# Moving operands of the matrix products start at other byte offsets than the weights

## The chip, the cores and the metric

The kernel runs on one core of a Trainium2 chip. The metric is the device time of one execution in microseconds (us); lower is better. Before the change two runs took 3464.58 and 3474.01 us, median 3469.3.

## The reference

Two networks run one after the other on a sequence of 512 tokens of width 1024, in float32. The first has four layers, each a token mixer (a gated linear recurrence, a gated unit that mixes chunks of 128 tokens, a short convolution, and the recurrence again) and a squared-ReLU MLP of width 4096. The second has one layer: a projection that feeds a delta-rule recurrence in chunks of 64 tokens and a dilated attention, then cross-attention over 256 memory rows, then another squared-ReLU MLP. What most of the time goes to is this:

```python
def _sqrelu_mlp(h, w1, w2):
    return jnp.square(jax.nn.relu(h @ w1)) @ w2
...
        h = _rmsnorm(x, norm_mix_g[i])
        ...
        x = x + mix
        x = x + _sqrelu_mlp(_rmsnorm(x, norm_mlp_g[i]), mlp_w1[i], mlp_w2[i])
...
        n = rmsnorm(h, norm_mix_g[l])
        proj = (n @ w_in[l]).astype(f32)
        ...
        u = rmsnorm(h, norm_ffn_g[l]) @ ffn_w1[l]
        h = h + (jnp.square(jax.nn.relu(u)) @ ffn_w2[l]).astype(h.dtype)
```

## The kernel before

Activations stay in SBUF, features on the 128 partitions and the 512 tokens along the row: `x` is the residual stream, 8 tiles of 128 features by 512 tokens. Every large product is made of three: weights and activations are each split into an upper part in the type float32r and the rest, also float32r, and the kernel adds upper*upper, upper weights*lower activations and lower weights*upper activations in PSUM. The upper and lower parts of the weights are `wh` and `wl`; those of the normed input are `xh` and `xl`, those of the MLP's activation `hh` and `hl`. Other inputs of products have pairs of their own: `yh`/`yl` (mixer outputs), `mh`/`ml` (memory), `rh`/`rl`, `oh`/`ol`, `gdh`/`gdl`, `yah`/`yal`.

Weights come in units of 1024 rows by 256 columns. SyncE's queue brings a unit into one of two slots of `raw` (L422), ScalarE rounds it to `wh` (L433), VectorE subtracts to get `wl` (L438), and TensorE multiplies (L501): for each of 8 row tiles and 2 column tiles one instruction for each of the three products, so 48 to a unit. In each, 128x128 weights are loaded into the array, and 512 columns of the activation stream past them. A few stages are swapped (L476): the activation is loaded, and 256 columns of the weights stream past it. Loads and streams are separate instructions; the load for the next product runs beside the stream of this one. Semaphores order everything: `landed`, `upper`, `lower` and `units` for the weights' two slots, `split` for activation tiles as they become ready, `evac` for PSUM banks.

After a stage of the kind `fin` VectorE adds PSUM to `x` (L671), ScalarE writes a tile of `xh` (L594), and VectorE one of `xl` (L681). After a stage of the kind `relu` VectorE writes `tmp` (L660), POOL squares it into `hf` (L617), ScalarE squares it into `hh` (L584), and VectorE writes `hl` (L666). Groups that repeat run as loops in which a register holds the tile's address.

Memory is laid out by hand. `pers` (L101) places tensors one after another, from `raw` to `c128`; `at` (L140) places tensors at offsets in KiB from `ARENA` (L137), which is moved up to the offset of the weights modulo 512 bytes. `xh` and `xl` are persistent, and their space is also that of the chunked recurrence, by `XH_AT`. As all the tensors from `wh` to `xl` have sizes that are multiples of 512 bytes, and a row tile of an activation is 2048 bytes, every float32r operand on either side of a product begins at the same byte modulo 512 in this kernel. Behind `tmp`, whose 4160 bytes are 8 x 512 + 64, the small tensors of the list (`hf` is the first of them) stand at other offsets.

Of the kernel before, what the change touches and what calls it, by code (L numbers as in the profile page):

```python
# [10 lines left out]
F32R = mybir.dt.float32r  # L11

P = 128
T = 512
D = 1024
ND = D // P
# [8 lines left out]
NC = T // CH  # L25
NH2 = 8
MEM = 256
NEG = 1e30
KIB = 1024
# [65 lines left out]
def build(nc, a, out):  # L95
# [5 lines left out]
    def pers(name, shape, dt=F32):  # L101

        n = 4
        for s in shape[1:]:
            n *= s
        off = used[0]
        used[0] += (n + 31) // 32 * 32
        return nc.alloc_sbuf_tensor_at(name, shape, dt, offset=off)
# [8 lines left out]
    wl = pers("wl", [P, 2, 8, 256], F32R)  # L117
    x = pers("x", [P, ND, T])
    XH_AT = used[0]
    xh = pers("xh", [P, ND, T], F32R)  # L120
    xl = pers("xl", [P, ND, T], F32R)
    ident = pers("ident", [P, P])
    ones = pers("ones", [P, P])
    headones = pers("headones", [P, P])
# [6 lines left out]
    prm = [pers(f"prm{i}", [P, P]) for i in range(4)]  # L131
# [8 lines left out]
    def at(name, kib, shape, dt=F32, base_at=None):  # L140
        n = 4
        for s in shape[1:]:
            n *= s
        off = (ARENA if base_at is None else base_at) + int(kib * KIB)
        assert base_at is not None or off + n <= LIMIT, (name, off + n, LIMIT)
        return nc.alloc_sbuf_tensor_at(name, shape, dt, offset=off)


    hh = at("hh", 0, [P, 16, T], F32R)
    hl = at("hl", 32, [P, 16, T], F32R)  # L150
    yh = at("yh", 40, [P, NR, T], F32R)
    yl = at("yl", 60, [P, NR, T], F32R)
    xtok = at("xtok", 0, [P, 4, D])
# [45 lines left out]
    w2a2 = at("w2a2", 88, [P, D])  # L199
    wda = at("wda", 92, [P, T])  # L200
    PCt = at("PC", 94, [P, NC, NH2])
    PCs = at("PCs", 94.25, [P, NC, NH2])
    XT_AT = XH_AT - 16 * KIB
    rt = at("rt", 0, [P, 8, T], base_at=XT_AT)

# [37 lines left out]
    stx = at("stx", 92, [P, 2, 16])  # L243
    mjunk = at("mjunk", 73, [P, D])

    fo = at("fo", 64, [P, ND, T])

    ps = [ctx.enter_context(nc.psum_tensor(f"ps{i}", [P, T], F32)) for i in range(8)]

# [2481 lines left out]
```

## Time and profile before

| | |
|---|---|
| two runs | 3464.58 and 3474.01 us, median 3469.3 |
| the profiled execution | span 3463.6 us, from the first to the last instruction; a time of its own beside the span isn't given, the lower run is 1.0 us above it |
| TensorE (PE) busy | 3370.7 us, 97% |
| weight loads (PEld) busy | 2754.4 us, 80% |
| VectorE, ScalarE, POOL busy | 1764.5, 1162.7 and 467.8 us |
| mean granted TensorE clock | 0.992 of full |
| DMA | 329.56 MB, mean 95 GB/s |

TensorE's matrix instructions are pipelined, so the time that one "takes" in the profile overlaps the next one, and TensorE is called busy throughout. What tells how fast it works is the distance from the start of one instruction to the start of the next. The timeline shows starts to 0.01 us, so this document takes them over many instructions.

### The profile page before, as it was taken

Reading aid. Unit: us, or ns where it says so; the run is one execution under the profiler, and the core shown is the slowest. Engines: PE = TensorE matmul, PEld = TensorE weight load, DVE = VectorE, ACT = ScalarE, POOL = GpSimd, SP = SyncE. Lnnn points to the kernel's source line nnn. Section 1 sums busy time; section 2 is a strip of 40 time slices with the busy share of each in tenths; the row PEclk is TensorE's granted clock in tenths of the full one; section 3 lists DMA queues with packets and bytes.
Section 4 is the critical chain, followed back from the end, with each engine's and each line's share of the span. In section 5 each row is a group of like instructions: output and inputs, shape, how many; then the busy total and the mean of one; then the engine's idle time right before and its main releaser. Section 6 shows DMA issues by size and latency. Waiting matters only on the chain. (4 is left out here: it accounts for less than half of the span.)

```text
span 3463.6 us, 51738 instructions
## 1 busy us (share of the span) xinstructions
PE 3370.7 (97%) x21556; PEld 2754.4 (80%) x21556; DVE 1764.5 (51%) x1954; ACT 1162.7 (34%) x1455; POOL 467.8 (14%) x417
## 2 busy tenths in 40 slices
PE   7999999999999999999999999999998889999998
PEld 5588888888888888887588888788776878878887
DVE  7764343454344554345765253655686555555342
ACT  3532123432222232222532123334563543332122
POOL 2011011020011021011011012000141221111011
PEclk9999999999999999999999999999999999999999
DMA  4233333233322233233233323343332122313232
GB/s 131 72 105 99 97 97 97 86 97 97 97 97 86 96 101 105 87 103 109 69 98 97 98 96 109 102 133 115 100 96 91 41 65 86 122 61 100 94 98 72
DMA packets 313270, 329.56 MB, mean 95 GB/s; under 512 B 22786, under 2 KB 304389, under 8 KB 312581
## 3 DMA queue, kind: packets, MB, share of 16 engines
q1 hardware_dynamic: 306325, 303.39, 27.6%
q0 software_dynamic: 4464, 19.40, 1.7%
q10 hardware_dynamic: 2304, 4.20, 0.3%
q8 instruction: 137, 2.24, 0.3%
q14 instruction: 40, 0.33, 0.0%
HBM read 312.28 MB, written 14.68 MB: 94 GB/s over the span
## 5 line engine op out<-in xcount | busy, mean ns | idle before, releaser
L501 PE MATMUL ps<-xh,wh 128*128 128x512 f32 x2360 | 930.6, 394 | 10.5 <-DVE wl L438 10.5
L501 PE MATMUL ps<-xh,wl 128*128 128x512 f32 x2360 | 920.1, 390 | 0.0
L501 PE MATMUL ps<-xl,wh 128*128 128x512 f32 x2360 | 919.7, 390 | 0.0
L438 DVE TENSOR_TENSOR wl<-raw,wh 128x2048 fp32r<-128x2048 f32 (+2 forms) x281 | 634.0, 2256 | 423.0 <-ACT wh L433 422.3
L433 ACT ACTIVATE wh<-raw 128x2048 fp32r<-128x2048 f32 (+1 forms) x284 | 526.9, 1855 | 668.7 <-PE ps L501 641.8
L501 PEld LDWEIGHTS ps<-xh,wh 128*128 128x128 f32 x2360 | 444.1, 188 | 115.9 <-issue 22.8
L501 PEld LDWEIGHTS ps<-xl,wh 128*128 128x128 f32 x2360 | 444.1, 188 | 95.2 <-issue 4.3
L501 PEld LDWEIGHTS ps<-xh,wl 128*128 128x128 f32 x2360 | 443.7, 188 | 93.1
L501 PE MATMUL ps<-hh,wh 128*128 128x512 f32 x1280 | 498.5, 389 | 1.2 <-DVE wl L438 0.9
L501 PE MATMUL ps<-hh,wl 128*128 128x512 f32 x1280 | 498.0, 389 | 0.0
L501 PE MATMUL ps<-hl,wh 128*128 128x512 f32 x1280 | 498.0, 389 | 0.0
L617 POOL TENSOR_TENSOR hf<-tmp 128x512 f32<-128x512 f32 x160 | 163.3, 1042 | 1133.6 <-DVE tmp L660 1133.6
L584 ACT ACTIVATE hh<-tmp 128x512 f32 (+1 forms) x160 | 97.7, 633 | 598.7 <-DVE tmp L660 598.7
L501 PEld LDWEIGHTS ps<-hh,wh 128*128 128x128 f32 x1280 | 240.3, 188 | 52.3 <-DVE wl L438 2.4
L501 PEld LDWEIGHTS ps<-hh,wl 128*128 128x128 f32 x1280 | 240.3, 188 | 50.0
L501 PEld LDWEIGHTS ps<-hl,wh 128*128 128x128 f32 x1280 | 240.3, 188 | 49.6
L660 DVE SCALAR_TENSOR_TENSOR tmp<-ps,rs 128x512 f32<-128x512 f32 x160 | 103.0, 686 | 341.2 <-PE ps L501 341.1
L671 DVE TENSOR_TENSOR x<-x,ps 128x512 f32 (+1 forms) x128 | 82.2, 684 | 355.8 <-PE ps L501 355.8
L630 POOL TENSOR_TENSOR acc<-acc,hf 128x512 f32<-128x512 f32 x80 | 118.4, 1480 | 1016.7 <-ACT hf L596 1012.8
L666 DVE TENSOR_TENSOR hl<-hf,hh 128x512 f32 (+1 forms) x160 | 158.4, 1029 | 55.4 <-POOL hf L617 55.4
L594 ACT ACTIVATE xh<-x,prm (+1 forms) x72 | 51.6, 717 | 273.0 <-DVE x L671 273.0
L501 PE MATMUL ps<-yh,wh 128*128 128x512 f32 x352 | 137.4, 390 | 0.0
(426 smaller groups left out, 3680.2 us busy)
## 6 DMA issues: line engine op xcount, KB each, us to landing
raw<-in_mlp_w SPq DMA_DIRECT2D x128, 1024.0 KB, 5.4
raw<-in_ffn_w SPq DMA_DIRECT2D x32, 1024.0 KB, 5.2
raw<-in_w_in SPq DMA_DIRECT2D x31, 1024.0 KB, 5.3
raw<-in_a_w_in SPq DMA_DIRECT2D x20, 1024.0 KB, 5.1
raw<-in_c_w_in SPq DMA_DIRECT2D x12, 1024.0 KB, 5.1
raw<-in_a_w_out SPq DMA_DIRECT2D x16, 640.0 KB, 4.0
raw<-in_b_w_in SPq DMA_DIRECT2D x8, 1024.0 KB, 5.7
raw<-in_xa_wkv SPq DMA_DIRECT2D x8, 1024.0 KB, 6.0
```

The costliest lines, as they stand in the source:

```text
L433: nc.scalar.activation(wh[:, p.slot(su), 0:n], raw[:, p.slot(su), 0:n], ACT.Copy).then_inc(upper, 1)
L438: nc.vector.tensor_tensor(wl[:, p.slot(su), 0:n], raw[:, p.slot(su), 0:n], wh[:, p.slot(su), 0:n], ALU.subtract).then_inc(lower, 1)
L501: last = nc.tensor.matmul(banks[mt][:, 0:st.n], stat_, ops[oi][at_, kk, 0:st.n], start=k == 0 and su == 0 and n_ == 0, stop=k == kb - 1 an ...
L584: nc.scalar.activation(hh[:, bass.ds(t, 1)], tmp[:, mt:mt + 1, 0:T], ACT.Square).then_inc(acted, 1)
L594: nc.scalar.activation(xh[:, bass.ds(t, 1)], x[:, bass.ds(t, 1)], ACT.Copy, scale=gaincol(st, t)).then_inc(acted, 1)
L617: nc.gpsimd.tensor_tensor(hf[:, mt], tmp[:, mt, 0:T], tmp[:, mt, 0:T], ALU.mult).then_inc(pooled, 1)
L630: nc.gpsimd.tensor_tensor(acc[:], acc[:], sq[:, mt], ALU.add).then_inc(pooled, 1)
L660: nc.vector.scalar_tensor_tensor(out=tmp[:, mt, 0:T], in0=ps[b + mt][:], scalar=0.0, in1=rs[:], op0=ALU.max, op1=ALU.mult).then_inc(evac, 1)
L666: nc.vector.tensor_tensor(hl[:, bass.ds(t, 1)], hf[:, mt:mt + 1], hh[:, bass.ds(t, 1)], ALU.subtract).then_inc(split, 1)
L671: nc.vector.tensor_tensor(xt, xt, ps[b + mt][:].rearrange("p (a n) -> p a n", a=1), ALU.add).then_inc(evac, 1)
```

## The change

`xh` starts 256 bytes, `xl` 16, `hh` 32 and `hl` 384 bytes past the weights' offset modulo 512. To make room, the space of `xh` and `xl` grows by 544 bytes; what stands behind it in the list moves up by 544 bytes (32 modulo 512), and the arena by 512. `PCs`, a small table of the recurrence, moves into columns of `prm3` that nothing uses, and `fo`, the tensor of the final norm, up by 1 KiB. Sizes, arithmetic, semaphores and the number of products are untouched; `yh`, `yl` and the other pairs keep their offset modulo 512.

```diff
--- before.py
+++ after.py
@@ -117,8 +117,11 @@
     wl = pers("wl", [P, 2, 8, 256], F32R)
     x = pers("x", [P, ND, T])
     XH_AT = used[0]
-    xh = pers("xh", [P, ND, T], F32R)
-    xl = pers("xl", [P, ND, T], F32R)
+    OFF = dict(xh=256, xl=16, hh=32, hl=384)
+    xspace = pers("xspace", [P, 2 * ND * T + (512 + 32) // 4], F32R)
+    xh = nc.alloc_sbuf_tensor_at("xh", [P, ND, T], F32R, offset=XH_AT + OFF["xh"])
+    xl_space = nc.alloc_sbuf_tensor_at("xl", [P, OFF["xl"] // 4 + ND * T], F32R, offset=XH_AT + ND * T * 4 + 512)
+    xl = xl_space[:, OFF["xl"] // 4:OFF["xl"] // 4 + ND * T].rearrange("p (k t) -> p k t", t=T)
     ident = pers("ident", [P, P])
     ones = pers("ones", [P, P])
     headones = pers("headones", [P, P])
@@ -146,8 +149,8 @@
         return nc.alloc_sbuf_tensor_at(name, shape, dt, offset=off)
 
 
-    hh = at("hh", 0, [P, 16, T], F32R)
-    hl = at("hl", 32, [P, 16, T], F32R)
+    hh = at("hh", OFF["hh"] / KIB, [P, 16, T], F32R)
+    hl = at("hl", 32 + OFF["hl"] / KIB, [P, 16, T], F32R)
     yh = at("yh", 40, [P, NR, T], F32R)
     yl = at("yl", 60, [P, NR, T], F32R)
     xtok = at("xtok", 0, [P, 4, D])
@@ -199,7 +202,7 @@
     w2a2 = at("w2a2", 88, [P, D])
     wda = at("wda", 92, [P, T])
     PCt = at("PC", 94, [P, NC, NH2])
-    PCs = at("PCs", 94.25, [P, NC, NH2])
+    PCs = prm[3][:, 64:P].rearrange("p (c q) -> p c q", c=NC)
     XT_AT = XH_AT - 16 * KIB
     rt = at("rt", 0, [P, 8, T], base_at=XT_AT)
 
@@ -243,7 +246,7 @@
     stx = at("stx", 92, [P, 2, 16])
     mjunk = at("mjunk", 73, [P, D])
 
-    fo = at("fo", 64, [P, ND, T])
+    fo = at("fo", 65, [P, ND, T])
 
     ps = [ctx.enter_context(nc.psum_tensor(f"ps{i}", [P, T], F32)) for i in range(8)]
 
```

Instructions on TensorE, ScalarE, POOL and SyncE are the same, in the same order. `xl` is now a slice that begins 16 bytes inside its tensor, and on VectorE this adds one register instruction for each of its writes in loops, 28 in the program, each of which runs twice. The place is the end of the loop body of a stage of the kind `fin`, on VectorE, before:

```order
L671 TENSOR_TENSOR x<-x,ps 128x512
L671 ISA
L671 TENSOR_TENSOR x<-x,ps 128x512
L676 REGISTER_ALU
L681 ISA
L681 SCALAR_TENSOR_TENSOR xl<-x,prm_62,xh 128x512
L676 REGISTER_ALU
L681 ISA
L681 SCALAR_TENSOR_TENSOR xl<-x,prm_62,xh 128x512
```

and in the changed kernel (lines are 3 further down):

```order
L674 TENSOR_TENSOR x<-x,ps 128x512
L674 ISA
L674 TENSOR_TENSOR x<-x,ps 128x512
L679 REGISTER_ALU
L684 ISA
L684 REGISTER_ALU
L684 SCALAR_TENSOR_TENSOR xl<-x,prm_63,xh 128x512
L679 REGISTER_ALU
L684 ISA
L684 REGISTER_ALU
L684 SCALAR_TENSOR_TENSOR xl<-x,prm_63,xh 128x512
```

A `REGISTER_ALU` now stands between the register work of L684 and the `SCALAR_TENSOR_TENSOR` that writes `xl`, in both halves of the body; nothing else moved.

## Rows read from the trace of the kernel before

**Rows 1.** The page: its head and the busy time of each engine.
```profile
span 3463.6 us, 51738 instructions
PE 3370.7 (97%) x21556; PEld 2754.4 (80%) x21556; DVE 1764.5 (51%) x1954; ACT 1162.7 (34%) x1455; POOL 467.8 (14%) x417
```

**Rows 2.** Waits of PE: line, releaser, total us, times, longest us.
```profile
PE ps L501 <- DVE wl L438: 14.5, 8, 3.1
...
PE ps L476 <- DVE xl L681: 1.8, 2, 1.1
```

**Rows 3.** Groups of PE by shape: busy us, mean ns, idle before.
```profile
L501 PE MATMUL ps<-xh,wh 128*128 128x512 f32 x2360 | 930.6, 394 | 10.5 <-DVE wl L438 10.5
...
L501 PE MATMUL ps<-xl,wh 128*128 128x512 f32 x2360 | 919.7, 390 | 0.0
L501 PE MATMUL ps<-hh,wh 128*128 128x512 f32 x1280 | 498.5, 389 | 1.2 <-DVE wl L438 0.9
...
L476 PE MATMUL ps<-wh,xh 128*128 128x256 f32 x224 | 64.9, 290 | 6.8 <-DVE wl L438 5.0 <-DVE xl L681 1.8
```

**Rows 4.** Timeline of PE, 28 products in a row: start us, duration us.
```profile
499.67 0.39 PE L501 MATMUL ps<-hl,wh 128*128 128x512 f32 x1
...
505.79 0.39 PE L501 MATMUL ps<-hl,wh 128*128 128x512 f32 x1
```

**Rows 5.** Timeline of PE, 15 swapped products of 256 columns in a row.
```profile
624.77 0.28 PE L476 MATMUL ps<-wh,xl 128*128 128x256 f32 x1
...
626.45 0.28 PE L476 MATMUL ps<-wh,xh 128*128 128x256 f32 x1
```

**Rows 6.** Timeline of PE at the lower clock, and its window (PEclk third last).
```profile
649.13 0.63 PE L501 MATMUL ps<-xh,wh 128*128 128x512 f32 x1
...
650.41 0.60 PE L501 MATMUL ps<-xh,wh 128*128 128x512 f32 x1
...
649.50:650.40 0.90, 0.90 (x3) 0.67 (x2) 0.00 (x0) 0.90 (x1) 0.00 (x0) 0.50 1.09 387
```

**Rows 7.** Timeline of PE after another product, at the higher clock, and its window.
```profile
124.62 0.39 PE L501 MATMUL ps<-xl,wh 128*128 128x512 f32 x1
...
125.08 0.40 PE L501 MATMUL ps<-xh,wh 128*128 128x512 f32 x1
125.32 0.39 PE L501 MATMUL ps<-xl,wh 128*128 128x512 f32 x1
125.54 0.39 PE L501 MATMUL ps<-xh,wl 128*128 128x512 f32 x1
...
126.93 0.39 PE L501 MATMUL ps<-xh,wl 128*128 128x512 f32 x1
...
129.19 0.39 PE L501 MATMUL ps<-xh,wh 128*128 128x512 f32 x1
...
124.70:129.40 4.70, 4.70 (x22) 3.86 (x21) 3.94 (x7) 4.65 (x7) 0.00 (x0) 1.00 0.52 179
```

**Rows 8.** Timeline of PE: plain float32 products, one and fifteen merged.
```profile
3046.43 0.59 PE L2342 MATMUL ps<-ptx,vx 128*128 128x512 f32 x1
...
3047.73 6.60 PE L2342 MATMUL ps<-ptx,vx 128*128 128x512 f32 x15
```

**Rows 9.** Line L1604: duration min/median/max ns, first and last start us.
```profile
L1604 PE MATMUL ps<-rt,headones x8: 590/590/591, 2491.8 to 2607.2; 128*128 128x512 f32 x8
...
L1604 PE MATMUL ps<-hf,headones x8: 590/590/591, 2510.3 to 2624.9; 128*128 128x512 f32 x8
```

**Rows 10.** What feeds a unit: groups of ACT and DVE, and DMA issues.
```profile
L433 ACT ACTIVATE wh<-raw 128x2048 fp32r<-128x2048 f32 x264 | 504.2, 1910 | 652.7 <-PE ps L501 626.3 <-DMA raw<-in_a_w_in 13.8 <-PE ps L476 11.7
...
L438 DVE TENSOR_TENSOR wl<-raw,wh 128x2048 fp32r<-128x2048 f32 x261 | 603.5, 2312 | 411.7 <-ACT wh L433 411.0
...
raw<-in_mlp_w SPq DMA_DIRECT2D x128, 1024.0 KB, 5.4
```

**Rows 11.** Line L681, its register instructions: duration min/median/max ns.
```profile
L681 DVEq FUSED_REGOPS  x56: 80/80/86, 519.3 to 3101.4; - x56
```

## The prediction, made before the changed kernel was run

> **What bounds the kernel now.** I read the page's busy times first: TensorE is busy 97% of the span, VectorE 51% [rows 1]. The waits of TensorE come next. The largest on another engine in the steady stages is 14.5 us in eight pieces, for a split of weights [rows 2], so nothing but its own pace holds TensorE up. What it works on is in the groups by shape: the streams of `xh` and `hh` [rows 3], each of which stands there three times with the same count (upper*upper, upper*lower, lower*upper). Durations of 390 ns overlap there, so the pace has to be read from starts. In the timeline 27 steps from 499.67 to 505.79 us [rows 4] give 0.2267 us for a product of 512 columns, and 14 steps from 624.77 to 626.45 [rows 5] give 0.1200 us for one of 256. The difference is 106.7 ns for 256 columns, 0.417 ns each, which is the upper level of the clock, 2.4 GHz. So 512 columns stream in 213.3 ns, 256 in 106.7, and in both cases **13.3 ns are left over for each product**. These are all the change can speak to.
>
> Three rows say what kind of time that is. At the lower clock (1.2 GHz, granted 0.50) three steps from 649.13 to 650.41 make 0.427 us each [rows 6], exactly 512 columns and nothing over. Plain float32 products come at (6.60 - 0.59)/14 = 429.3 ns [rows 8], twice 213.3 and 2.6 over: they ask for the stream at half the rate and lose next to nothing. And the left-over isn't constant. When the stream starts again behind another stage, at full clock (granted 1.00), ten steps from 124.62 to 126.93 us take 231 ns each, single ones between 0.22 and 0.24, and only then do they settle, with ten steps of 226 from 126.93 to 129.19 [rows 7]. The operands and their addresses modulo 512 are the same before and after settling. A fixed price of changing weights would not wander. Something depends on how the load of the next weights and the running stream meet in time, and it ends in a locked rhythm at 226.7.
>
> That is the question of this change: whether they also meet by address. If so, new offsets move the rhythm to which it locks. If they meet by time alone, nothing changes.
>
> **The change, part by part.** Products touched: 3 x 2360 with `xh` and `xl` and 3 x 1280 with `hh` and `hl`, of 512 columns, 10,920 in all, and 3 x 224 = 672 swapped ones [rows 3]. They take 10,920 x 0.2267 + 672 x 0.120 = 2475 + 81 = 2556 us, 74% of the span. Each ns on all 11,592 is 11.6 us. One per cent is 3 ns; 2%, 69 us, is 6.0 ns. About 2% is also what a measurement of this kernel can tell from no change, and I use it as that.
>
> It passes through in full both ways. A unit of weights is 48 products, 10.9 us; its supply is 5.4 us of transfer, 1.9 of ScalarE and 2.3 of VectorE [rows 10], in two slots. The last two, which follow the release of a slot, take 4.2 us while the other slot is multiplied. Even at 213.3 ns a unit would last 10.2 us, and the same slack would cover them.
>
> The price of the new offsets for a product isn't in this trace, since no float32r product here has another. Bounds: the slowest and fastest single steps of the same products, 0.24 and 0.22 us [rows 7], which are +13.3 and -6.7 ns on the settled pace (+154 and -77 us in all). Beyond the fast end lies the left-over of the plain float32 product, 2.6 instead of 13.3 ns, worth 10.7 x 11,592 = 124 us. I take 0. The nearest row on address is L1604: its stream of `rt` begins at the weights' offset and that of `hf` 64 bytes past it (4160 bytes of `tmp` are 8 x 512 + 64), and both take 590 ns, minimum to maximum within 1 ns [rows 9]. It is a weak row, for these are plain float32, which lose little anyway. The second reason is the 13.3 ns themselves: the same for streams of 512 and 256 columns [rows 4, 5], in which `xh` is once the stream and once what is loaded. A clash by address would have to cost the same in both roles and at both lengths.
>
> The Trainium skill (TensorE: Matmul & The Clock Gate, "Step-by-step: what each phase is for") says that TensorE reads its stream and its weights through two independent ports of SBUF, so that loading the next weights takes nothing from the running product; by that rule offsets can't matter either, and the time stays. The same page ("Back-to-back issue gap") puts products of 512 columns 215.8 ns apart, with which the trace does not agree: 226.7 [rows 4], so the rule of independent ports does not explain the left-over either.
>
> The rest costs nothing. VectorE runs 28 x 2 = 56 more register instructions; the nearest, 80 ns each [rows 11], would make 4.5 us, below it 0. They hide in VectorE's idle half, and TensorE waits for `xl` only twice, 1.8 us [rows 2]; uncovered there, they add 0.2 us. `xh`, `xl`, `hh` and `hl` are written at new offsets; if that slowed ScalarE or VectorE, the tiles' slack before the eighth row tile (7 x 6 x 0.227 = 9.5 us into the next stage) covers it. The small tensors move by 32 bytes, the arena by 512, `PCs` and `fo` elsewhere; the products on them are plain float32, for which rows 9 stand.
>
> Sum: 3463.6 + 0. The median of the runs is 5.7 us above that span, the lower run 1.0; I forecast **3468 us**.
>
> **Rivals.**
> 1. *No effect of address*, the forecast, chance 0.46. For it: rows 9, and one left-over for two lengths and roles. Against: the wandering of rows 7.
> 2. *The rhythm locks at a worse place*, slower. Place: the stream of every product in rows 3, beside the load of the next weights. In the mild form the products run as before they settle, 231 ns: +4.3 x 11.6 = +50 us, 3519, chance 0.15. In the hard one they lock at the slow end, 0.24: +154 us, 3624, chance 0.12. It decides from 6 ns on average, that is 233. For it: the unsettled steps are slower on average than the settled ones, so a place taken blindly is likelier worse than better. Four different offsets average out, against the hard form.
> 3. *It locks at a better place.* Between 0.22 and the present pace: down to -77 us, in the middle -39 us, 3431, chance 0.15, a third of it beyond 2%. For it: a step of 0.22 exists.
> 4. *The meeting goes away*, and the left-over falls to 2.6 ns: 3468 - 124 = 3344, chance 0.12. For it: rows 6 and 8 show that it vanishes once the stream asks for less, so it isn't needed for changing weights. Against: four unlike offsets would all have to be good ones.
>
> Likely enough too is a mixture, one operand better and one worse; it lies between these.
>
> **How the numbers follow.** Within 2%: 0.46 + nearly all of the mild slow form (0.13) + two thirds of rival 3 (0.10) = 0.69. Faster by over 2%: 0.12 + 0.05 = 0.17. Slower by over 2%: 0.12 + 0.02 = 0.14. The range goes from 3375, which leaves most of rival 4 out (0.10), to 3550, which leaves most of the hard slow form out (0.10). The forecast's own range is 3455 to 3482.
>
> **What would show it.** The distance between starts for each kind of stream: `xh` (256), `xl` (16), `hh` (32), `hl` (384), and `yh` as one that keeps its offset. If rival 1 is right, all are at 226.7, and the steps of rows 7 repeat. If address counts, `yh` stays at 226.7 and others leave it, each for itself; then the kernel's time must move by the sum of their counts times their differences. A swapped product of 256 columns tells whether it counts which side is offset. If the time moves while all distances stay, I am wrong in another way: then waits of TensorE for `wl` or `xl` must have grown beyond rows 2. What would make the prediction wrong is mainly that the left-over is a meeting by address, which this trace can't exclude.

## The result

The changed kernel took 3511.03 and 3512.88 us, median 3511.95, against 3469.3 before: ratio 1.0127, 95% interval 1.0109 to 1.0146. It is 1.3% slower, 43 us. None of the executions of the kernel before that were timed beside the experiments took more than 3476.24 us, so this is clear of noise. The forecast was 3468, no change; what came is nearest to rival 2 in its mild form, which had 3519.

The page of the changed kernel says at once what it is not:

```profile
span 3509.3 us, 51794 instructions
PE 3420.2 (97%) x21556; PEld 2751.8 (78%) x21556; DVE 1767.8 (50%) x1954; ACT 1162.7 (33%) x1455; POOL 470.4 (13%) x417
```

Compared with [rows 1] TensorE is busy 49.5 us longer with the same number of products, and the other engines are within 3.3 us of what they were. The groups of TensorE by shape (busy us, mean ns of one, idle before):

```profile
L504 PE MATMUL ps<-xh,wh 128*128 128x512 f32 x2360 | 939.0, 398 | 9.4 <-DVE wl L441 9.2
L504 PE MATMUL ps<-xl,wh 128*128 128x512 f32 x2360 | 930.4, 394 | 0.0
L504 PE MATMUL ps<-hl,wh 128*128 128x512 f32 x1280 | 504.8, 394 | 0.0
L504 PE MATMUL ps<-hh,wh 128*128 128x512 f32 x1280 | 502.0, 392 | 0.7 <-DVE wl L441 0.7
L504 PE MATMUL ps<-yh,wh 128*128 128x512 f32 x352 | 137.5, 391 | 0.0
```

All four streams that moved are 3 to 5 ns longer than in [rows 3], and than the row of `hl` in the same view of the kernel before:

```profile
L501 PE MATMUL ps<-hl,wh 128*128 128x512 f32 x1280 | 498.0, 389 | 0.0
```

The wait for the split of weights has not grown (9.2 us before `xh`, 10.5 in [rows 3]). The starts tell the pace. In the timeline of `xh` and `xl`, 24 products apart, then of `hh` and `hl`, 21 apart (start us, duration us):

```profile
1319.79 0.39 PE L504 MATMUL ps<-xl,wh 128*128 128x512 f32 x1
...
1323.27 0.39 PE L504 MATMUL ps<-xl,wh 128*128 128x512 f32 x1
...
1325.35 0.40 PE L504 MATMUL ps<-xl,wh 128*128 128x512 f32 x1
```
```profile
503.06 0.39 PE L504 MATMUL ps<-hl,wh 128*128 128x512 f32 x1
...
507.90 0.40 PE L504 MATMUL ps<-hl,wh 128*128 128x512 f32 x1
```

That is 5.56/24 = 0.2317 and 4.84/21 = 0.2305 us, where [rows 4] had 0.2267. The first stretch lies deep inside a stage, long after the ten or so products in which the kernel before settled [rows 7]; the second begins with the second product of its stage. The changed kernel does settle, but not on one step: for `xh` and `xl` it repeats a series of 15 steps between 224 and 241 ns, and for `hh` and `hl` one of 9 between 227 and 238. One round of the first is 1319.79 to 1323.27 us, 3.48/15 = 0.2320; a round of the second is 2.08 us, 0.2311 a step.

Taken over the whole trace from start to start (those of 300 ns and more, which are waits and the lower clock, left out), in ns:

| kernel | xh | xl | hh | hl | yh |
|---|---|---|---|---|---|
| before | 226.9 | 226.8 | 226.8 | 226.6 | 226.9 |
| the change | 232.2 | 231.7 | 230.1 | 233.2 | 227.1 |
| x_only | 232.2 | 231.7 | 226.7 | 226.9 | 226.9 |
| h_only | 226.9 | 226.8 | 232.0 | 229.4 | 226.9 |
| space_only | 226.8 | 226.8 | 226.7 | 226.7 | 226.9 |
| all_160 | 234.3 | 234.3 | 234.3 | 234.3 | 227.0 |
| all_256 | 226.9 | 226.8 | 226.8 | 226.6 | 226.9 |

(The labels are those of the experiments below. A distance is booked on the product that begins it, so within a stage of mixed products the columns share: all products with `xh` and `xl` together stand at 232.0 in the change, those with `hh` and `hl` at 231.1, against 226.9 and 226.7 before.) `yh`, which kept its offset, kept its pace. The sum closes: the steps below 300 ns of the line of these products (L501, L504 in the change) took 2876.4 us in the change and 2820.4 before, +56.0; its longer steps, waits and the lower clock, 57.5 against 67.3, -9.8; swapped products -0.5; the rest +0.4. Together +46, the difference of the spans (3509.3 - 3463.6 = 45.7).

### The profile page after: what moved, and what is told of

Same layout as the page of the kernel before. It is cut to its first block, busy times and chain, and to the rows that moved or that the text cites. A ratio compares the mean times of both kernels' runs of the same rounds, so it can differ in the third digit from the quotient of the medians.

```text
span 3509.3 us, 51794 instructions
## 1 busy us (share of the span) xinstructions
PE 3420.2 (97%) x21556; PEld 2751.8 (78%) x21556; DVE 1767.8 (50%) x1954; ACT 1162.7 (33%) x1455; POOL 470.4 (13%) x417
## 4 chain that ended last, share of the span: by engine, by line
PE 93%; DVE 3%; ACT 2%; issue 1%; SPq 0%; POOL 0%; DMA 0%; POOLq 0%; DVEq 0%; ACTq 0%
PE ps L504 81%; PE ps L479 2%; PE ps L980 2%; PE ps L1920 1%; PE ps L1949 1%; DVE wl L441 1%; PE ps L1921 0%; ACT wh L436 0%; PE ps L1860 0%; PE ps L2316 0%; PE ps L2345 0%; DVE cX L2136 0%; PE ps L1876 0%; PE ps L1885 0%; PE ps L535 0%
## 5 line engine op out<-in xcount | busy, mean ns | idle before, releaser
L504 PE MATMUL ps<-xh,wh 128*128 128x512 f32 x2360 | 939.0, 398 | 9.4 <-DVE wl L441 9.2
L504 PE MATMUL ps<-xh,wl 128*128 128x512 f32 x2360 | 934.3, 396 | 0.0
L504 PE MATMUL ps<-xl,wh 128*128 128x512 f32 x2360 | 930.4, 394 | 0.0
L504 PEld LDWEIGHTS ps<-xh,wh 128*128 128x128 f32 x2360 | 443.7, 188 | 125.1 <-issue 21.3
L504 PEld LDWEIGHTS ps<-xl,wh 128*128 128x128 f32 x2360 | 443.4, 188 | 109.6 <-issue 4.3
L504 PEld LDWEIGHTS ps<-xh,wl 128*128 128x128 f32 x2360 | 443.4, 188 | 103.2
L504 PE MATMUL ps<-hl,wh 128*128 128x512 f32 x1280 | 504.8, 394 | 0.0
L504 PE MATMUL ps<-hh,wh 128*128 128x512 f32 x1280 | 502.0, 392 | 0.7 <-DVE wl L441 0.7
L504 PE MATMUL ps<-hh,wl 128*128 128x512 f32 x1280 | 502.6, 393 | 0.0
L504 PEld LDWEIGHTS ps<-hh,wh 128*128 128x128 f32 x1280 | 239.7, 187 | 59.5 <-DVE wl L441 1.9
L504 PEld LDWEIGHTS ps<-hl,wh 128*128 128x128 f32 x1280 | 240.4, 188 | 55.3
L504 PEld LDWEIGHTS ps<-hh,wl 128*128 128x128 f32 x1280 | 240.4, 188 | 53.8
L504 PE MATMUL ps<-yh,wh 128*128 128x512 f32 x352 | 137.5, 391 | 0.0
```

Of the source, the lines that this page charges most:

```text
L504: last = nc.tensor.matmul(banks[mt][:, 0:st.n], stat_, ops[oi][at_, kk, 0:st.n], start=k == 0 and su == 0 and n_ == 0, stop=k == kb - 1 an ...
```

## The experiments

**The halves of the change, and what stands around it.** Three kernels, each the changed one with one line edited; all were timed in three rounds against the kernel before.

```diff
-    OFF = dict(xh=256, xl=16, hh=32, hl=384)
+    OFF = dict(xh=256, xl=16, hh=0, hl=0)      # x_only
+    OFF = dict(xh=0, xl=0, hh=32, hl=384)      # h_only
+    OFF = dict(xh=0, xl=0, hh=0, hl=0)         # space_only
```

> xh and xl at 256 and 16, hh and hl back at 0. Both theories: the streams of xh and xl keep the changed kernel's mean of about 233 ns, those of hh and hl return to 226.7 and lock. Of the changed kernel's +43 us about two thirds stay: near 3500 us, ratio to the kernel before 1.009. If the pace were set by something shared (the moved arena, the small tensors), hh and hl would stay at 231.

> hh and hl at 32 and 384, xh and xl back at 0. The other third: near 3485 us, ratio 1.0045; hh and hl at 231.5 ns, xh and xl at 226.7. The two halves add up to the whole change.

> The rest of the change alone: the space grows, the small tensors move by 32 bytes and the arena by 512, PCs and fo move, but all four offsets are 0. Theories 1 and 2: 3469 us, ratio 1.000 within 0.002, every float32r stream at 226.7. A rival, that the move of the small tensors or the tables slows the kernel: 3512 us here too.

Measured: x_only 3498.26 us, ratio 1.0094 (1.0077 to 1.0111); h_only 3481.39 us, ratio 1.0045 (1.0028 to 1.0062); space_only 3467.67 us, ratio 0.9999 (0.9989 to 1.0009). One of the ten executions of space_only took 19,219 us and is left out of its ratio; nothing on record says why. The halves add to 1.0139, within the interval of the whole. In x_only, 47 products of a stage of `xh` and `xl`, then the same stage in h_only, in the timeline:

```profile
1319.80 0.39 PE L504 MATMUL ps<-xh,wh 128*128 128x512 f32 x1
...
1330.71 0.39 PE L504 MATMUL ps<-xh,wl 128*128 128x512 f32 x1
```
```profile
1319.76 0.39 PE L504 MATMUL ps<-xl,wh 128*128 128x512 f32 x1
...
1330.41 0.39 PE L504 MATMUL ps<-xh,wh 128*128 128x512 f32 x1
```

10.91/47 = 0.2321 against 10.65/47 = 0.2266 us. Every pair of streams goes by its own offsets. The moved small tensors, the arena, `PCs`, `fo` and the space cost nothing. The 56 register instructions are not part of space_only, whose `xl` is no slice inside its tensor (51,738 instructions against 51,794); x_only and the change have them, and TensorE's wait for `xl` is 2.0 us there against 1.8 before.

**A map of offsets.** A short program with only such products, in the kernel's order of upper, lower, upper. A table gives the offsets, and each of its lines is a line of the source, by which the profile names it:

```python
CONFIGS = [    # stream upper, stream lower, weights, in bytes
    (0, 0, 0, lambda *a, **k: NC[0].tensor.matmul(*a, **k)),     # L16
    (16, 16, 0, lambda *a, **k: NC[0].tensor.matmul(*a, **k)),   # L17
...
                for k in range(8):
                    for mt in range(2):
                        for n_, (wt, oi) in enumerate(((0, 0), (0, 1), (1, 0))):
                            wa = ow // 4 + wt * 2048 + k * 256 + mt * 128
                            ma = offs[oi] + k * 512
                            last = mm(banks[mt][:], w[:, wa:wa + 128], m[:, ma:ma + 512], start=k == 0 and n_ == 0, stop=k == 7 and n_ == 2)
```

> Leaves out the whole computation: only products of this kind run, 144 for each pair of offsets (48 by 3, in the kernel's order of upper, lower, upper), one source line for each pair; the output is a copy of the input. Offsets: all streams alike from 0 to 496 bytes in steps of 16, also 4 and 8, unlike pairs such as 256 and 16, and weights moved along. Theory 1 (each product's own distance in bytes between its stream and its weights sets its pace): a curve over the offset when all streams are alike, with 226.7 ns at 0 and other values elsewhere, 256/16 near 233 and 32/384 near 231.5 as in the changed kernel; 64/64 with weights at 64 gives 226.7 again. Theory 2 (unlike neighbours break the rhythm): every common offset gives 226.7, only the unlike pairs 229 to 234. Either way 512 past reads as 0. If neither 256/16 nor 32/384 leaves 226.7 here, the pace is not a matter of addresses alone.

Groups by line. As the durations overlap without a hole, busy time less one duration, over the count less one, is the pace. In the order shown, stream upper/lower/weights are 0/0/0, 16/16/0, 64/64/0, 160/160/0, 256/256/0, 272/272/0, 4/4/0, 256/16/0, 32/384/0, 256/0/0, 64/64/64 and 0/0/64:

```profile
L16 PE MATMUL ps<-mall,wall 128*128 128x512 f32 x144 | 32.8, 389 | 0.0
...
L17 PE MATMUL ps<-mall,wall 128*128 128x512 f32 x144 | 33.5, 394 | 0.0
...
L20 PE MATMUL ps<-mall,wall 128*128 128x512 f32 x144 | 33.1, 391 | 0.0
...
L26 PE MATMUL ps<-mall,wall 128*128 128x512 f32 x144 | 33.9, 396 | 0.0
...
L32 PE MATMUL ps<-mall,wall 128*128 128x512 f32 x144 | 32.8, 389 | 0.0
...
L33 PE MATMUL ps<-mall,wall 128*128 128x512 f32 x144 | 33.5, 394 | 0.0
...
L48 PE MATMUL ps<-mall,wall 128*128 128x512 f32 x144 | 34.4, 400 | 0.0
...
L50 PE MATMUL ps<-mall,wall 128*128 128x512 f32 x144 | 33.6, 394 | 0.0
...
L51 PE MATMUL ps<-mall,wall 128*128 128x512 f32 x144 | 33.4, 393 | 0.0
...
L52 PE MATMUL ps<-mall,wall 128*128 128x512 f32 x144 | 32.9, 389 | 0.0
...
L58 PE MATMUL ps<-mall,wall 128*128 128x512 f32 x144 | 32.8, 389 | 0.0
...
L60 PE MATMUL ps<-mall,wall 128*128 128x512 f32 x144 | 33.8, 395 | 0.0
```

So (32.8 - 0.389)/143 = 226.7 ns at 0. Busy times are given to 0.1 us, so the rows leave half a ns open; taken from start to start, the pace is 231.6 at 16, 229.0 at 64, 234.3 at 160, 237.5 at 4, and 226.9 at 256, where it comes to 226.7 after its first products; 272 reads as 16, and so on through all multiples of 16 up to 496: the map **repeats every 256 bytes**. The change's own pairs come out at 232.0 (256/16) and 231.1 (32/384), as the two pairs together have in the kernel (232.0 and 231.1). It is the distance to the weights that counts and no address of its own: 64/64 is good again when the weights stand at 64 too (L58), and bad streams result from moving the weights alone (L60); with the weights at 448, which puts the streams 64 past them modulo 256, the pace is 228.9, as with the streams at 64 (L20). 256/0 is as good as 0/0, so of the change's first pair the 16 does the harm and the 256 none. Theory 2 (only unlike neighbours) falls with L17 to L26, where both streams have the same offset.

**All starts, all pairs, and whose weights.** The same program with the streams at every multiple of 4 bytes, with upper and lower weights at different offsets, and with all 256 pairs of multiples of 16.

```diff
-            for oh, ol, ow, mm in CONFIGS:
+            for oh, ol, ow, ov, mm in CONFIGS:      # ov: the lower weights' own offset
```

> Leaves out the whole computation: 96 products for each set of offsets, one source line each; the output is a copy of the input. Part one: both streams alike at 4 to 252 bytes past the weights in steps of 4 (the first map repeated every 256 bytes, so this covers all). By the first map the multiples of 16 come out at 226.7 only for 0 and 240, elsewhere 229 to 234.6; starts that are no multiple of 16 are expected above those, as 4 bytes gave 237.5. Part two: upper and lower weights at different offsets. Theory 1a (a product's own weights count): upper stream 0, lower stream 64, upper weights 0, lower weights 64 is bad, since the product lower stream by upper weights is 64 off. Theory 1b (the weights that are being loaded beside the stream count, that is the next product's): the lower stream runs while the lower weights are loaded, so this set has distance 0 everywhere and gives 226.7, while all streams at 0 with only the lower weights at 64 does not.

> Leaves out the whole computation: 48 products for each of 256 pairs of offsets of the upper and the lower stream, 0 to 240 in steps of 16; the output is a copy of the input. Open: whether any unlike pair is below 226.7. If 226.7 is a floor of the rhythm, none is, and it is reached where both are 0 or 240. If the left-over can be avoided, some pair goes towards 216.

Groups by line of the first: streams at 100, then (stream 0, lower stream 64, weights 0, lower weights 64), and all at 0:

```profile
L41 PE MATMUL ps<-mall,wall 128*128 128x512 f32 x96 | 23.2, 403 | 0.0
...
L80 PE MATMUL ps<-mall,wall 128*128 128x512 f32 x96 | 22.3, 393 | 0.0
L89 PE MATMUL ps<-mall,wall 128*128 128x512 f32 x96 | 21.9, 389 | 0.0
```

(23.2 - 0.403)/95 = 240.0 ns is the worst, at 100 (also at 132, 196 and 244). Of starts that are no multiple of 16, those 12 past one were nearly always the best (227.7 to 233.3, against my guess that all would be worse), those 4 past one mostly the worst. Theory 1b falls: with L80 every stream has distance 0 to what is loaded beside it, and it still takes 231.1 from start to start. By 1a it is bad, which agrees. But if each product had a price by its own distance, the lower stream alone at 64 would make the mean of 226.7, 229.0 and 226.7, that is 227.5; measured (L84) it is 232.0. So neither rule of pairs gives the numbers. Only all starts alike modulo 256 settled at 226.7 every time.

And the pace isn't a function of these offsets alone. With both streams at 240 the first map, which came to it from 224, ran at 226.7; the second, which came from 236, at 236.6; and the program of pairs, which came from 240/224, at 233.3, each for as long as it lasted. The last two have the same memory layout and differ in what ran before (in the first map the lower weights also stand 1 KiB nearer), so an offset can have more than one rhythm, and which one comes depends on more than the offset. Among the 256 pairs the last 24 products of each gave 226.7 for 0/0 and for two more (112/240 and 192/16), 242 at most (128/112), 231.7 as the median, and nothing below 226.7. If an offset that is a multiple of 16 could shorten the left-over, this would likely have shown it.

**The dose.** The changed kernel with all four at 160, the map's 234.3, and with all four at 256, the map's 226.7.

```diff
-    OFF = dict(xh=256, xl=16, hh=32, hl=384)
+    OFF = dict(xh=160, xl=0, hh=160, hl=160)    # all_160, with xl's own tensor at + 160
+    OFF = dict(xh=256, xl=0, hh=256, hl=256)    # all_256, with xl's own tensor at + 256
```

> The whole kernel with xh, xl, hh and hl all 160 bytes past the weights, where the first map has 234.3 ns. If the map holds in the kernel, 10,920 products take 7.6 ns more each: +83 us on 3467, so 3550 us, ratio 1.024, and hh, hl, xh and xl all stand at 234.3. If unlike neighbours were the cause, alike offsets would cost nothing: 3467.

> The whole kernel with xh, xl, hh and hl all 256 bytes past the weights: not at the weights' offset modulo 512, but at it modulo 256. The maps repeat every 256 bytes, so this must be the kernel before: 3467 us, ratio 1.000 within 0.002, every stream at 226.7. If the first map's period were an accident of the short program, it is slower, like the change.

Measured: all_160 3535.62 us, ratio 1.0202 (1.0185 to 1.0219), 69 us on the kernel before in its rounds; all_256 3467.67 us, ratio 0.9998 (0.9986 to 1.0009). In the timelines, 47 products of the same stage of all_160 and of all_256:

```profile
1319.75 0.40 PE L504 MATMUL ps<-xh,wl 128*128 128x512 f32 x1
...
1330.76 0.39 PE L504 MATMUL ps<-xl,wh 128*128 128x512 f32 x1
```
```profile
1319.77 0.39 PE L504 MATMUL ps<-xh,wl 128*128 128x512 f32 x1
...
1330.42 0.39 PE L504 MATMUL ps<-xl,wh 128*128 128x512 f32 x1
```

11.01/47 = 0.2343 and 10.65/47 = 0.2266 us, both as the short program had them. That the time moved by 69 us and not by the 83 of the products is in the trace too: the steps below 300 ns took 86 us more (5 of them because 23 more steps are below 300 ns), waits and steps at the lower clock 14 less (53.1 against 67.3), products of other lines 5 less. Some of that is chance: the steps of these products at the lower clock took 20.4 us before, 11.5 in all_160 and 38.8 in space_only, whose products have the offsets of the kernel before. But not all of it, since in every slower kernel the median moved by less than the products' counts times what each grew by: 31 of 36 us in x_only, 14 of 17 in h_only, 43 of 53 in the change, 69 of 81 in all_160. That slower products leave their feeders more time is an argument, and no run shows it.

**Swapped products.** Here the activation is loaded and 256 columns of weights stream.

```diff
-                            last = mm(banks[mt][:], w[:, wa:wa + 128], m[:, ma:ma + 512], ...)
+                            last = mm(o, m[:, ma:ma + 128], w[:, wa:wa + 256], ...)
```

> Leaves out the whole computation: swapped products (the activation is loaded, 256 columns of the weights stream), 96 for each set of offsets; the output is a copy of the input. In the changed kernel these went from 120.0 to about 117.7 ns, so offset 0 is not the best for them. Expected: 120.0 at 0, a curve with values below 120 at some offsets, 117.7 at 256/16.

Groups by line: activations at 0, at 64, and at 256/16:

```profile
L16 PE MATMUL ps<-wall,mall 128*128 128x256 f32 x96 | 11.7, 283 | 0.0
...
L20 PE MATMUL ps<-wall,mall 128*128 128x256 f32 x96 | 11.0, 276 | 0.0
...
L39 PE MATMUL ps<-wall,mall 128*128 128x256 f32 x96 | 11.5, 281 | 0.0
```

Read from starts inside each line, 120.0, 113.3 and 117.8 ns. For this form 0 is among the worst offsets tried and 64 the best, only 6.7 ns over its 106.7 of streaming. In the change the swapped products of `xh` and `xl` went from 119.9 to 117.8 ns, so they gained 1.4 us. A version with the weights of swapped stages at 64 and those of the others at 0 would gain 864 x 6.7 = 5.8 us, an estimate from these rows, 0.17%. It wasn't tried: it needs room behind the weight buffers, in a memory where even the change had to move `PCs` and `fo`.

**What the left-over is made of.** The short program at fixed offsets with other numbers of columns, and with other types.

```diff
+    ("r", 0, 512, 32, lambda ...),    # float32r, offset 0, 512 columns stream, 32 columns of weights loaded
+    ("f", 4, 512, 128, lambda ...),   # plain float32, offset 4
+    ("b", 64, 512, 128, lambda ...),  # bfloat16, offset 64
```

> Leaves out the whole computation: 96 products for each case, one source line each; the output is a copy of the input. What makes up the left-over of 13.3 ns at offset 0. Theory A (the load of the next weights takes time from the stream, 16 bytes of weights a cycle of 0.417 ns: 512 bytes are 32 cycles, 13.3 ns): with 96, 64 and 32 columns of weights the left-over falls to 10, 6.7 and 3.3 ns. Theory B (a fixed price for each product): it stays 13.3. Both: streams of 480, 448, 384, 320 and 256 columns leave the same 13.3. Types: plain float32 at 429.3 ns at every offset, and bfloat16 (half the bytes) near 216 at every offset, since the stream asks SBUF for less; if address matters for these as well, they spread by several ns.

Groups by line: 128, 64 and 32 columns of weights at offset 0; 64 columns at offset 160; a stream of 480 columns; plain float32 at offset 0 and 4:

```profile
L16 PE MATMUL ps<-mall,wall 128*128 128x512 f32 x96 | 21.9, 389 | 0.0
...
L24 PE MATMUL ps<-mall,wall 128*64 128x512 f32 x96 | 22.2, 392 | 0.0
L25 PE MATMUL ps<-mall,wall 128*32 128x512 f32 x96 | 22.4, 394 | 0.0
...
L27 PE MATMUL ps<-mall,wall 128*64 128x512 f32 x96 | 21.9, 389 | 0.0
...
L18 PE MATMUL ps<-mall,wall 128*128 128x480 f32 x96 | 21.0, 378 | 0.0
...
L29 PE MATMUL ps<-raw 128*128 128x512 f32 x192 | 82.6, 592 | 0.0
L30 PE MATMUL ps<-raw 128*128 128x512 f32 x192 | 82.6, 592 | 0.0
```

Both theories fall. At offset 0 the pace gets worse with fewer columns of weights, 230.0 at 96 and 64 and 231.7 at 32, instead of better (A) or equal (B). At offset 160 it gets better: 234.3 with 128 columns, 230.7 with 96, 226.7 with 64 (L27, once settled), 230.5 with 32. So the number of columns moves the rhythm as an offset does, in either direction. Streams of 384, 320 and 256 columns settle with 13.3 ns left over, but 448 and 480 leave 16.0 and 16.6. Plain float32 is at 429.2 at 0, 64 and 160 and 429.5 at 4, as expected. bfloat16 stands at 216 from start to start at every offset that is a multiple of 16 (a few of its records are missing, so its rows give less well); at 2 and 4 bytes single steps of up to 221 appear, and the mean is 217.0 and 216.1. Only float32r at the full clock cares by more than about 1 ns.

What stays open is the mechanism itself: why the meeting has a period of 256 bytes, and what carries over from one product to the next. These are rhythms of stream and load that these runs map and do not explain.

## Why the prediction was wrong

**Right:** that TensorE's pace sets the time; the counts; that the left-over was no fixed price, since it wandered after a stop [rows 7]; that the rest of the edit costs nothing (space_only), and the register instructions 0.2 us. The size of the mild form of rival 2, taken from the unsettled products, came near: 231 ns forecast, 232.0 and 231.1 found. That its +50 us stand so close to +43 is in part luck: the products of 512 columns cost more than it said, 53 us by their counts and not 47, the swapped ones became faster and not slower, and not all of the cost reached the end, where the prediction had it pass through in full.

**Wrong:** the step "I take 0" for the price of the new offsets. Measured, the price is 5.1 ns on each product with `xh` and `xl` and 4.4 on each with `hh` and `hl`. The 0 rested on two things. One was L1604, plain float32 at 0 and 64 bytes [rows 9]. The last experiment shows that this row could not have said anything: plain float32 stays within 0.3 ns at every offset tried. I called it weak and let it decide. The other was that 13.3 ns stood at both lengths and in both roles [rows 4, 5]. That was a coincidence of offset 0. Elsewhere the two part: at 64 the swapped product falls to 113.3 while the normal one rises to 229.0. Why an offset costs what it costs stays open.

**What should have weighed more** was in the prediction already. The same operands at the same addresses went through steps of 0.22 to 0.24 us and settled near the lowest of them [rows 7]. A pace that depends on when stream and load meet may well depend on where they meet too. And since the settled value lay well below the mean of the unsettled ones, a blind move was likelier to lose. The prediction asked the first and wrote the second, and gave a slower rhythm 0.27. That is an argument after the fact; rows 7 could not have proved it.

The Trainium skill (TensorE: Matmul & The Clock Gate, "Step-by-step: what each phase is for") says that through two independent read ports the load of the next weights takes no read bandwidth from the running product. That offsets therefore can't matter, as the prediction drew from it, does not hold for float32r streams: 226.7 to 240.0 ns by offset alone. The page's formula for an isolated product ("Back-to-back issue gap") gives 215.8 ns for 512 columns; the bfloat16 products here, each with a load beside it, stand at 215.8, the float32r ones at 226.7 or more.

Neither of the other rivals came: no pair of 256 was below 226.7, so for the normal form these offsets had nothing to gain.

## What to carry to other kernels

Where float32r streams at full clock bound a kernel, start both operands of every product of 128x128 weights and 512 columns at the same byte modulo 256; it is worth 1 to 13 ns of 227 to a product here, and costs padding alone. Read the pace from starts over some dozens of products, per operand, and take a pace that wanders after a stop as a reason to test the layout. For another form of product (operands swapped, fewer columns of weights) map the offsets anew: swapped, 64 was better than 0, and with 64 columns of weights 160 was better than 0.

## What the runs showed of the hardware that I had not expected

- The pace of float32r products repeats with the offset every 256 bytes, from 226.7 to 240.0 ns where all streams start alike, and depends on the distance between stream and weights, not on addresses (64/64/64: 226.7, 0/0/64: 233.3).
- A rhythm can be a series of 9 or 15 unequal steps that repeats exactly (the change), and one offset can have several, each stable for as long as it was run: 226.7, 233.3 and 236.6 ns at 240.
- Loading fewer columns of weights quickens it or slows it, by the offset: 226.7, 230.0, 230.0 and 231.7 ns for 128, 96, 64 and 32 columns at 0, and 234.3, 230.7, 226.7 and 230.5 at 160.
- 256 columns of weights streaming past an activation take 113.3 ns at 64 bytes and 120.0 at 0.
